# Scores ahead of turning in both attentions, and branch products of the first block as three rounded passes

## The reference, cut to what matters

```python
merged = jax.nn.sigmoid(u @ w_gate[l, 0]) * (y_a @ w_branch[l, 0])
merged = merged + jax.nn.sigmoid(u @ w_gate[l, 1]) * (y_b @ w_branch[l, 1])
merged = merged + jax.nn.sigmoid(u @ w_gate[l, 2]) * (y_c @ w_branch[l, 2])
merged = merged + jax.nn.sigmoid(u @ w_gate[l, 3]) * (y_d @ w_branch[l, 3])
h = h + merged @ w_o[l]
```

## Time and profile before

| | |
|---|---|
| runs | 2848.41, 2851.09, 2851.96 us; median 2851.09 |
| the profiled execution | 2854.93 us, its span 2853.1 us |
| TensorE busy | 2778.7 us |
| VectorE busy | 1836.1 us |
| ScalarE busy | 1360.9 us |
| mean granted clock of TensorE | 0.992 of full speed |

### The profile page before, as it was taken

The page is one execution under the profiler, slowest core; times in us unless marked ns, Lnnn a source line. Parts: engine busy times, 40 slices in busy tenths (PEclk is TensorE's granted clock), DMA queues, the critical chain, the costliest instruction groups (busy, mean ns, idle before and its releaser), DMA issues.

```text
span 2853.1 us, 41544 instructions
## 1 busy us (share of the span) xinstructions
PE 2778.7 (97%) x16646; PEld 2413.1 (85%) x16646; DVE 1836.1 (64%) x2800; ACT 1360.9 (48%) x1946; POOL 103.9 (4%) x135
## 2 busy tenths in 40 slices
PE   7999999999999999999999999998999998999998
PEld 6888988888888988888878889996888888988787
DVE  5666566566766656756676665554667666655666
ACT  4554444355455444435445544444545454453444
POOL 1000000000000000001011001110000000000000
PEclk9999999999999999999999999999999999999999
DMA  6454333445455543346445545453444454434443
GB/s 243 180 200 167 142 144 140 174 159 188 175 189 185 194 172 129 140 155 230 178 180 194 183 175 170 154 171 122 178 183 173 181 195 159 164 146 155 171 182 125
DMA packets 49044, 488.43 MB, mean 171 GB/s; under 512 B 6480, under 2 KB 6576, under 8 KB 10520
## 3 DMA queue, kind: packets, MB, share of 16 engines
q1 hardware_dynamic: 43192, 470.44, 44.8%
q0 software_dynamic: 5728, 16.25, 2.0%
HBM read 485.47 MB, written 1.19 MB: 171 GB/s over the span
## 4 chain that ended last, share of the span: by engine, by line
PE 88%; DVE 6%; ACT 3%; issue 1%; DMA 1%; POOL 0%; DVEq 0%; ACTq 0%; POOLq 0%
PE ps L855 68%; PE ps L915 15%; DVE ring_lo L1852 2%; ACT ring_hi L1496 1%; PE ps L1129 1%; PE ps L871 1%; PE ps L1333 1%; DMA norm_g<-norm_gT_dram 1%; DVE ring_lo L1865 1%; PE ps L1348 1%; PE ps L1240 0%; ACT ring_hi L1547 0%; DVE xn L1981 0%; DVE ring_lo L1908 0%; DVE h L1963 0%
## 5 line engine op out<-in xcount | busy, mean ns | idle before, releaser
L855 PE MATMUL ps<-uT,ring_hi 128*128 128x512 f32 (+1 forms) x5536 | 1519.8, 346 | 10.3 <-DVE qkT L2011 9.3
L855 PE MATMUL ps<-uT,ring_lo 128*128 128x256 f32 x4176 | 1177.7, 282 | 0.0
L855 PEld LDWEIGHTS ps<-uT,ring_hi 128*128 128x128 f32 x5536 | 958.7, 191 | 160.2 <-issue 18.0
L855 PEld LDWEIGHTS ps<-uT,ring_lo 128*128 128x128 f32 x4176 | 795.8, 191 | 6.2
L1945 DVE TENSOR_TENSOR ring_lo<-ring,ring_hi 128x2048 fp32r<-128x2048 f32 x160 | 366.9, 2293 | 221.0 <-ACT ring_hi L1547 221.0
L1852 DVE TENSOR_TENSOR ring_lo<-ring,ring_hi 128x3072 fp32r<-128x3072 f32 (+1 forms) x110 | 330.6, 3006 | 177.3 <-ACT ring_hi L1496 177.2
L1496 ACT ACTIVATE ring_hi<-ring 128x3072 fp32r<-128x3072 f32 (+1 forms) x110 | 273.5, 2487 | 300.9 <-PE ps L855 280.5
L1547 ACT ACTIVATE ring_hi<-ring 128x2048 fp32r<-128x2048 f32 x167 | 317.4, 1901 | 0.0
L915 PE MATMUL ps<-ring_hi,hid_hi 128*128 128x512 f32 x704 | 276.7, 393 | 0.0
L915 PE MATMUL ps<-ring_lo,hid_hi 128*128 128x512 f32 x704 | 275.9, 392 | 0.0
L915 PE MATMUL ps<-ring_hi,hid_lo 128*128 128x512 f32 x704 | 273.9, 389 | 0.0
(11 more groups left out here) (301 smaller groups left out, 2619.8 us busy)
## 6 DMA issues: line engine op xcount, KB each, us to landing
ring<-stream_dram SPq DMA_DIRECT2D x299, 1536.0 KB, 6.3
mlaT_all<-bias_vectors POOLq DMA_DIRECT2D x32, 96.0 KB, 2.8
bias<-gains_dram POOLq DMA_DIRECT2D x5, 512.0 KB, 7.5
yR<-bias_vectors POOLq DMA_DIRECT2D x1, 2048.0 KB, 11.1
mlaT_all<-bias_vectors POOLq DMA_DIRECT2D x32, 64.0 KB, 2.8
row<-ret_const_dram POOLq DMA_DIRECT2D x1, 1280.0 KB, 5.7
h<-x_rows_dram POOLq DMA_DIRECT2D x2, 512.0 KB, 11.8
yR<-gains_dram POOLq DMA_DIRECT2D x2, 512.0 KB, 9.8
```

The costliest lines, as they stand in the source:

```text
L855: m = pe.matmul(out_, lhsT, rhs, start=start, stop=stop, **kw)
```

## The change

The change splits all weights of the branch products (the MERGE kind is gone: its slots are WHOLE; slots 29 and 30, now with four tiles of 512 columns each, are split over 2048 columns), writes the low halves of the branch outputs (`low_outputs`, `low_diff` on VectorE, signalled by `branch_low`), and makes each branch product of three rounded passes. In both attentions the scores of a step are issued ahead of the turn of the pair before.

```diff
-RAW, WHOLE, MERGE, FFN = range(4)
+RAW, WHOLE, FFN = range(3)
 _FFN = [FFN] * C_FFN
-_MIX = ([WHOLE] * (C_A + 2) + [RAW] + [WHOLE] * 2 + [RAW] + [WHOLE] + [RAW] + [WHOLE] * 2 + [MERGE] * 8 + [FFN] + [MERGE] * 4
-        + [WHOLE] * 2 + [RAW] * 2 + [WHOLE] * (C_WO - 1) + [RAW])
+_MIX = ([WHOLE] * (C_A + 2) + [RAW] + [WHOLE] * 2 + [RAW] + [WHOLE] + [RAW] + [WHOLE] * 10 + [FFN] + [WHOLE] * 4
+        + [WHOLE] * 2 + [FFN] * 2 + [WHOLE] * (C_WO - 1) + [RAW])
...
-            return 2, m - 32, False, True, S_BRANCH_2 + (m - 32) // 6, ((m - 32) % 6) * 512
+            return 2, m - 32, False, True, S_BRANCH_2 + (m - 32) // 4, ((m - 32) % 4) * 512
...
-        SPLIT_STEPS = {0: T_SLOTS[4], 2: 12, 3: 13} | {t: t + 9 for t in range(5, 20)}
-        LATE_SPLITS = (0, 2)
+        SPLIT_STEPS = {0: T_SLOTS[4], 2: 12, 3: 13} | {t: t + 9 for t in range(5, 21)}
+        LATE_SPLITS = (0, 2, 20)
...
             kind = SLOT_KIND[c]
-            if kind == MERGE:
-                return x.rearrange("p (n w) -> p n w", n=2)[:, :, 0:D]
             return x[:, 0:2 * D] if kind == FFN else x
...
                 if t == 15:
-                    pe.wait_ge(branch_in, COPIES_LAYER * l + COPIES_OF_BRANCH[3])
+                    pe.wait_ge(branch_low, COPIES_LAYER * l + COPIES_OF_BRANCH[3])
...
             def attention(l):
                 for t in range(STEPS):
+
+                    if t < PAIRS:
+                        scores(l, t)
                     if 1 <= t <= PAIRS:
                         turn(l, t)
-                    if t < PAIRS:
-                        scores(l, t)
...
                 else:
-                    weights(c)
+                    split_weights(c)
                 if branch:
                     if ct == 0:
-                        pe.wait_ge(branch_in, COPIES_LAYER * l + COPIES_OF_BRANCH[b])
+                        pe.wait_ge(branch_low, COPIES_LAYER * l + COPIES_OF_BRANCH[b])
+                    n = b if b < 2 else 3 - b
                     for k in range(4):
-                        last = mm(bank[:, SEQ:2 * SEQ], slot(c)[:, o + k * P:o + (k + 1) * P], yT[b if b < 2 else 3 - b][:, k, :],
-                                  k == 0, k == 3)
+                        out_, cols = bank[:, SEQ:2 * SEQ], slice(o + k * P, o + (k + 1) * P)
+                        mm(out_, high(c)[:, cols], yT[n][:, k, :], k == 0, False)
+                        mm(out_, high(c)[:, cols], yT_low[n][k], False, False)
+                        last = mm(out_, low(c)[:, cols], yT[n][:, k, :], False, k == 3)
...
                 for s in range(NS2 + 1):
+                    if s < NS2:
+                        dilated_scores(s)
                     if s:
                         dilated_turn(s - 1)
-                    if s < NS2:
-                        dilated_scores(s)
...
                 gate(l, merge_at(2 * STEPS - 1))
-                take_high(mix_slot(l) + S_WO)
+                take_high(mix_slot(l) + S_BRANCH_2 + 1)
                 for k in range(K_SPLIT):
-                    if k == 4:
-                        take_high(mix_slot(l) + S_WO + 1)
+                    if k == 3:
+                        take_high(mix_slot(l) + S_WO)
                     act.wait_ge(merged, 32 * l + branches_before(32) + 1 + k)
                     act.activation(mTh[:, k, :], mT[:, k, :], ACT.Copy).then_inc(merged_hi, 1)
+                take_high(mix_slot(l) + S_WO + 1)
...
+            def low_of(l, n, place, src, high_):
+
+
+                dve.wait_ge(branch_in, COPIES_LAYER * l + n)
+                return dve.tensor_tensor(place, src, high_.bitcast(F32), ALU.subtract)
...
+            def low_outputs(l, t):
...
+            def low_diff(l):
+                for fp in range(2):
+                    src = ps[:, 2 + fp, :].rearrange("p (f t) -> p f t", f=2)
+                    if fp == 0:
+                        last = low_of(l, 9, row_r[:, :, 0:SEQ], src, yT[0][:, 0:2, :])
+                    else:
+                        low_of(l, 10, yT_low[0][2], src[:, 0, :].rearrange("p (a c) -> p a c", a=2),
+                               yT[0][:, 2, :].rearrange("p (a c) -> p a c", a=2))
+                        last = low_of(l, 10, yT_low[0][3], src[:, 1, :], yT[0][:, 3, :])
+                    last.then_inc(branch_low, 1)
...
+                    if t >= 2:
+                        low_outputs(l, t - 2)
                     compress(l, t)
                     add(2 * t)
                     if t == 13:
                         diff_norm(l, 2)
+                    if t == 14:
+                        low_diff(l)
...
+                take_low(mix_slot(l) + S_BRANCH_2 + 1)
                 for m in range(32, N_MERGE):
                     add_branch(l, m)
-                    if m == 32:
-                        take_low(mix_slot(l) + S_WO)
                     if m >= 34:
                         low_of_merged(m - 34)
+                    if m == 36:
+                        take_low(mix_slot(l) + S_WO)
```

More of the change, by code:

```diff
@@ L184, in build @@
         xn = sb("xn", [P, TT, D])
+        xn_r = nc.alloc_sbuf_tensor_at("xn_r", [P, TT * D], F32R, offset=nc.sbuf_base - TT * D * 4, align_bytes=32)
         uT = sb("uT", [P, KD, 2, SEQ], F32R)
@@ L192, in build @@
         row = sb("row", [P, TT, ROW_W])
+        row_r = nc.alloc_sbuf_tensor_at("row_r", [P, TT, ROW_W], F32R, offset=nc.sbuf_base - TT * ROW_W * 4, align_bytes=32)
         yR = sb("yR", [P, 4, TT, 512])
@@ L252, in build @@
         blk = flatY[:, 3072:4032].rearrange("p (l h c) -> p l h c", l=CMP_LEN, h=2)
-        yT = [flatY[:, o:o + 1024].rearrange("p (f t) -> p f t", f=4) for o in (0, 2048)]
+        yT = [yR_r[:, o:o + 1024].rearrange("p (f t) -> p f t", f=4) for o in (0, 2048)]
+        yT_low = [[row_r[:, 0, 0:SEQ], row_r[:, 1, 0:SEQ], row_r[:, :, SEQ:SEQ + P], xn_r[:, 768:1024]],
+                  [mlaT_r[:, 12 + f, :] for f in range(4)]]
         hidC = flatY[:, 1024:1084].rearrange("p (w n) -> p w n", w=2)
@@ L407, in build @@
         branch_in = sem("branch_in")
+        branch_low = sem("branch_low")
         blocks_ready = sem("blocks_ready")
@@ L1150, in values @@
                     if t == 8:
-                        pe.wait_ge(branch_in, copied + 8)
+                        pe.wait_ge(branch_low, copied + 8)
                     pT, w = pT_sb[:, 0, :], slice(P * (t - 8), P * (t - 7))
@@ L1158, in values @@
                 if not nsa and t >= 2:
-                    pe.wait_ge(branch_in, copied + t - 1)
+                    pe.wait_ge(branch_low, copied + t - 1)
                 if t == 12:
@@ L2419, in diff_norm @@
                                              ALU.mult, ALU.mult).then_inc(y_diff_ready, 1)
+            def low_of(l, n, place, src, high_):
+                dve.wait_ge(branch_in, COPIES_LAYER * l + n)
+                return dve.tensor_tensor(place, src, high_.bitcast(F32), ALU.subtract)
+            def low_outputs(l, t):
+                if branch_copy(t) is None:
+                    return
+                dst, src = branch_copy(t)
+                if t < 8:
+                    place = yT_low[t // 4][t % 4]
+                    if t == 2:
+                        src, dst = (x.rearrange("p (a c) -> p a c", a=2) for x in (src, dst[:, 0, :]))
+                    else:
+                        dst = dst[:, 0, :]
+                    low_of(l, t + 1, place, src, dst).then_inc(branch_low, 1)
+                else:
+                    f = t - 17
+                    low_of(l, 11 + f // 2, mlaT_r[:, 12 + f:14 + f, :], src.rearrange("p (f t) -> p f t", f=2),
+                           dst).then_inc(branch_low, 1)
+            def low_diff(l):
[3 more added lines that the diff above has]
+                        last = low_of(l, 9, row_r[:, :, 0:SEQ], src, yT[0][:, 0:2, :])
+                    else:
+                        low_of(l, 10, yT_low[0][2], src[:, 0, :].rearrange("p (a c) -> p a c", a=2),
+                               yT[0][:, 2, :].rearrange("p (a c) -> p a c", a=2))
+                        last = low_of(l, 10, yT_low[0][3], src[:, 1, :], yT[0][:, 3, :])
+                    last.then_inc(branch_low, 1)
             def scale_gate(l, m):
@@ L2762, in pack_stream @@
         some(wg, (5, 6, 7), D)
-        some(wb, range(6), 512)
-        some(wb, (6, 7), 512)
+        some(wb, range(4), 512)
+        some(wb, range(4, 8), 512)
         rows(x["w_o"][l])
```

## The result

The changed kernel takes 2825.09 us (median of 4 runs, 2821.94 to 2826.44), the kernel before in the same comparison 2850.67: a ratio of 0.991 (95% interval 0.989 to 0.993), 25.6 us less. The forecast was 2837.6 with a range from 2828 to 2846: the sign is right, the size is nearly double the 13.5 us that were forecast.

What follows compares the result with a forecast made beforehand. TensorE was taken as the bound, with VectorE time free. 12.7 - 2.2 - 4.2 + 2.9 + 4.3 = 13.5 us less than the median 2851.09 gave 2837.6; own range 2832 to 2842, wider range 2828 to 2846.

Steps and rivals of the forecast that it cites:

- rival (d): Loop steps: VectorE becomes the bound at the addition that frees the bank; slower, near 2884 us without slack; chance 0.07.
- step 15: First attention's loop: the turn waits 1.2 us instead of 0.2 for the low halves; 1.1 lost a layer, 2.2 in all.
- Behind the loop: TensorE waits 2.3 us for the output weights' split; output product 0.5 later; 2.1 lost a layer, 4.2 in all.
- boundary waits of the dilated attention: Dilated attention, pair boundaries: scores run ahead of the turn, the lost 0.49 us goes away at six boundaries, 2.9 us.
- the end of the dilated attention: Last dilated steps, up to the output product: scores done during the softmax, 4.3 us sooner, bound 0 to 5.3.
- A column tile of four products: Branch products: three passes of 0.120 us replace 0.426 us a product; 0.264 less a tile, 12.7 us over 48 in-loop tiles.
- the order only moves work: Both attentions: scores ahead of the turn change only waits; no gain counted in the first, 2.9 and 4.3 us in the dilated.
- the lower clock behind the loop: After the wait ahead of the output product: clock at 1.2 instead of 2.4 GHz, 1.6 us of work lost in each layer.
- rival (c): After the loop and at step 15: nothing stalls; 24.1 us less, 2827.0; chance 0.08.

Runs made afterwards that it cites:

- y_step15: Changed kernel with the copies and subtractions of the differential output moved ahead of the sigmoid and scaling of item 16: 2822.41 us.
- y_tail: Changed kernel with ScalarE's rounding and VectorE's splits behind the loop in another order: 2821.74 us.
- x_dilated: Kernel before with scores ahead of the turn in the dilated attention only, exact branch products kept: 2842.20 us.
- x_passes: Changed kernel with both orders put back (turn ahead of scores), so three passes alone: 2842.16 us.
- x_high_twice: Changed kernel whose middle pass reads the rounded branch output again instead of its low half, so its result differs from the reference: 2822.99 us.
- z_attention: Kernel before with scores ahead of the turn in the first block's attention only: 2845.52 us.
- z_odd: Kernel before with scores ahead of the turn in the odd steps of the dilated attention only: 2849.8 us, run once.
- y_both: Changed kernel with both new orders, that of the work behind the loop and that of step 15's copies and subtractions: 2817.80 us.
- y_two_passes: Changed kernel without the middle pass of every branch product, the low half still written by VectorE: 2811.54 us.
- z_even: Kernel before with scores ahead of the turn in the even steps of the dilated attention only: 2846.2 us, run once.

## Why the prediction was right and wrong

**Right.** TensorE sets the end, VectorE never held it in a loop step (rival (d)). At step 15 the wait is 1.60 us (forecast 1.2), for the low halves of the differential output, and y_step15 removes it. Behind the loop the stretch up to the output product is 0.52 us longer than before (forecast 0.5), with a wait of 2.37 (2.3) for the split of the output weights, of which y_tail takes 1.4 by another order. The boundary waits of the dilated attention are gone, 0.57 us each (0.49).

**Right in the number, in part by chance: the end of the dilated attention.** It is shorter by 4.3 us, as forecast. But the forecast held 5.3 for possible at full clock throughout and took less; measured, the end gave 4.3 with the clock at full speed, and 2.7 in x_dilated, where it fell behind the same wait. So 1.6 of the 4.3 us are a clock that stayed up, and what the order gives without the clock was set too high.

**Wrong, first: "A column tile of four products goes from 1.704 to 1.440 us, so 0.264 less."** Measured, from x_passes: 0.323, joints included. Both ends were off. The 13.63 us of the earlier trace rows hold 63 pitches of 0.216 and a last one of 0.028, since the output product begins right behind; two pitches, an exact product, are 0.431 us. And a pass does not take 0.120 everywhere but 0.114 to 0.120, by the tile that is streamed (x_high_twice). By the pitches alone a tile gains 1.72 - 1.43 = 0.29 or 1.72 - 1.38 = 0.34, 0.31 in the mean; the rest lies at the joints. 48 tiles: 15.5 us, not 12.7. The Trainium skill's "FP8 and Floating Point Precision" (TensorE Precision Notes) counts four passes for true FP32. The trace shows an exact product as two instructions and not its passes, so it doesn't settle the count. Three quarters of 0.431 would be 0.324, and this is not reached: three rounded passes take 0.345 or 0.357 in the mean of a tile.

**Wrong, second and larger: that the order only moves work.** What the order does to TensorE's own sequence had no term and no reason for leaving it out. The prediction priced the scores ahead of the turn by the waits they remove, nothing in the first attention and 2.9 + 4.3 in the dilated one. The runs showed 2.59 us in each loop (z_attention), of which 0.2 is a wait, and 0.20 in the dilated steps (z_odd), by the neighbours alone. This is 4.8 us in the first attention and 12 x 0.20 = 2.4 in the dilated one up to its end. The price could have been read from the trace of before: there the gates follow scores, as at 402.06 in the earlier trace rows, 0.306 us behind the last one, and in step 14 the transposes of the differential output, 0.028 us behind the last one (timeline, PE, the kernel before):

```profile
453.60 1.03 PE L1141 MATMUL ps<-cst,yR 128*128 128x128 f32 x8
454.39 0.49 PE L855 MATMUL ps<-uT,ring_hi 128*128 128x256 f32 x2
```

**Half: the lower clock behind the loop.** "I take this here too", for both layers. It came in one of two in the profiled execution, and cost 1.6 us as forecast.

**The sum again**, with what was measured: 13.5, and 2.8 for the tiles, 4.8 for the first attention's order, 3.0 for the dilated (10.2 by x_passes against after, not 7.2: 2.4 of the neighbours and 6 x 0.08 of the boundaries), 1.6 for one clock that stayed up, less 2 x 0.3 for step 15: 25.1 of the 25.6. This sum takes the clock as the profiled executions had it, and the 25.6 is a difference of medians, so that it closes within 0.5 us is more than it can promise. That rival (c) named 2827.0 is chance: its mechanism, no wait behind the loop, did not happen. The medians of the parts, 8.8 (x_passes), 4.7 (z_attention) and 8.7 (x_dilated), add to 22.2. The 3.4 that are left are about what two things make in the profiled executions: the wait of step 15 (1.60 with both in, not 2.30; 1.4 in two layers) and one clock that stayed up (1.6).

## What to carry to other kernels

Price a reordering by the starts of the instructions on both sides of every joint it makes or breaks, even where nothing waits: here 0.2 us in some 36 places, about 7 us, was more than the boundary waits that the order removed (3.4). Take a pitch from the middle of a stretch, not from its length, when the last one differs. And when an engine gets more splits, look first at what its neighbour stands idle for: moving two copies into a gap of 4.58 us, and one split ahead of two copies with VectorE's splits to match, gave a further 7 us. And before a shorter stretch is put down to an order, look at the granted clock in it: in the dilated end it was 1.6 of 4.3 us.

## What the hardware showed unexpectedly

The pitch of a rounded 256-column pass depends on the tile that it streams: 0.114 us from yR_r or mlaT_r behind the first four passes of a tile, near 0.120 with row_r and xn_r in between, at the same clock and with the same weights. Scores of 64 rows are followed by a rounded pass after 0.306 us and by a transpose after 0.307; transposes by a rounded pass after 0.028. The cause of either is open.

Whether the clock falls can't be told from one wait. Ahead of the output product, waits of 2.17 to 2.38 us were followed by the lower level (1.2 GHz) in 7 of 8 cases (after, x_passes, x_high_twice, y_step15), those of 0.99 us in none of 4 (y_tail, y_both); in y_two_passes one of 4.05 us was, one of 2.52 was not. At step 15 waits as long had another outcome: those of 2.30 us were followed by it in neither layer of x_passes, those of 2.46 in one of two (y_two_passes). The wait of 1.99 us ahead of the dilated pieces, the same in all thirteen traces, was followed by it in three: before, z_even and z_odd. At the dilated end the waits of 2.41 and 2.42 us were followed by it in z_even and x_dilated, and not in the seven traces with both new orders. In y_step15 the window behind the wait reads:

```profile
532.00:536.00 4.00, 3.71 (x11) 2.92 (x12) 3.52 (x10) 2.94 (x2) 0.00 (x0) 0.66 0.48 147
```

and the output part takes 25.16 us there against 23.59 in layer 0 of the changed kernel, with TensorE's work the same.
